# A fourth weight tile at the start, attention values made feature-major, and reordered queues in a two-layer float32 block

## The chip, the cores and the metric

The kernel runs on 1 core of one Trainium2 chip. The time is device microseconds of one launch. The kernel before takes 1545.37 us, the median of 3 runs (1543.23 to 1545.9).

## The reference

Two layers over 256 rows (T) of 1024 float32 features (D). Each layer: an RMS norm, one wide projection of the row, three mixers (MoBA attention, gated linear attention "GLA", mLSTM), each lifted by an up projection and gated, summed, projected by `w_o` and added to the row. Then a second norm and a feed-forward block: dense SwiGLU in layer 0, and in layer 1 a mixture of 8 experts, two per row, by a router.

```python
for l in range(DEPTH):
    h = rmsnorm(x, attn_norm_g[l])
    x = x + hybrid_mixer(h, w_in[l], b_in[l], ...)     # softmax attention | GLA | mLSTM, gates, w_o
    h = rmsnorm(x, ffn_norm_g[l])
    x = x + (swiglu(h, ...) if l % 2 == 0 else moe_swiglu(h, router_w[0], ...))
return rmsnorm(x, final_norm_g)
```

With 256 rows MoBA is plain causal softmax attention: 8 heads of 64.

## The kernel before, in words

**Numbers.** A weight is split in two float32r parts, high (a cast) and low (weight minus high); so is the activation. A product is three matmuls: high by high, high by low, low by high. All weights come as *chunks* of 128 x 2048 float32 (1 MB), in the order of use. A chunk is loaded by two transfers of 512 KB on the sync queue (`load`, `moe_loads`), cast on the scalar engine (ACT) into `w_hi` (`split_to` L1179, in the experts `split_moe` L1241), subtracted on the vector engine (DVE) into `w_lo` (L1521, in the experts L1665), and used by TensorE (PE): 24 matmuls of 512 columns in the dense part (`chunk`, L655 and L665; L644 is its form with 256 columns), 12 per chunk in the experts (L1100, L1111). `w_hi` and `w_lo` have 3 slots each (RS), the raw weights 3 slots in the dense part (RM, `raw_m`) and 11 in the experts (RE, `raw_m` and `late`). In the dense part the sync queue may load chunk g only when chunk g-3 has been split (`sp.wait_ge(lo_ready, g - RM + 1)`).

**Order.** Each engine has its own program, written out by hand, and runs it in order; a wait blocks all that stands behind it on that engine. `ahead(l, name, c)` on ACT and DVE means: split weights up to two chunks beyond chunk c of that unit. Engines wait on semaphores: `lo_ready` counts low parts, `full[b]` and `drained[b]` count the fills and the readings of PSUM bank b. The table `FILL`, made by `fills`, fixes which bank each result takes; PE's `claim` waits until the bank's last content is drained.

**Start.** The first two chunks (0 and 1, unit `mq`) come in five pieces (`PIECES`), each piece of x transposed (`front`, L439) followed by its weight piece (L441), all on the sync queue. Then chunk 2, `cols`, x by rows (`load_x`) and, after a wait for the first low part, chunk 3 into slot 0. The GpSimd (POOL) program waits for the last piece and then asks for biases, small weights and rope tables.

**A mixer layer.** PE runs units mq, mk, mv, gqk, gv, gr, lq, lk, lv, lo, g0 and so on, with small attention steps between them. MoBA: scores (L701), softmax without division, `prob_transposes` (L709), `prob_values` (L719, L725: rows of queries out, 64 columns per head), division by the row sums on DVE (`moba_rows`, L1630), and later `y_transposes(l, 0)` (L690), whose result is split into `yT_hi`/`yT_lo`. The mLSTM convolution (`conv_taps`, L1648) is 12 DVE operations for each of two halves, followed by a Silu on ACT.

**Router and experts.** Between the last `wo'` chunk and the first expert stand the logits (L1000, L1002), `lgT`, the ranks (L1035) and fillers (`keep_warm`, L1008, PSUM bank 3). DVE computes the picks, writes the selection matrix (`select`, L2013), the low rows (`rows_lo`, L1992), then `count_picks` (L1980 to L1984), which reads the `rank` bank for the last time at L1982. PE's `gather` (L1054) then writes 8 banks (`GBANKS`, the first is bank 0). The expert loop goes over `MS`: gate/up chunks ("gu", i, 0 and 1) and down chunks ("dn", i). After "gu" i is full, ACT writes the Silu (L1455), DVE `hid` (L2072), PE transposes it (L1078), ACT and DVE split it (L1460, L2083). `late_split` puts the split of chunk m+2 on DVE behind `hid` at "gu" i < 2. `gates_of_picks` (L1999 to L2007) stands at the first expert's third down chunk.

Of the kernel before, what the change touches and what calls it, by code (L numbers as in the profile page):

```python
# [12 lines left out]
def program(nc, x, front_d, b_in, cols_d, w_small_d, gate_w, dense_d, experts_d,  # L13
# [10 lines left out]
    P = 128  # L24
# [74 lines left out]
    for l in range(L):  # L99
        if l:  # L100
            fills(l, "norm", A4)
        for tag, banks in (
                ("mq", (0, 1)), ("rb", (5,)), ("mk", (2, 3)), ("small", (4,)), ("mv", (0, 1)),
                ("qkT", A4), ("gqk", (2, 3)), ("gv", (0, 1)), ("s0", A4), ("gr", (2, 3)), ("s1", A4),
                ("lq", (0, 1)), ("ga", (7,)), ("lk", (2, 3)), ("pT0", A4), ("lv", (0, 1)), ("pv0", (4, 5)),
# [12 lines left out]
    fills(1, "logits", (0,))  # L118
    fills(1, "lgT", (1,))
    fills(1, "rank", (0,))  # L120
# [68 lines left out]
    with ctx:  # L189
# [189 lines left out]
        p_ready = sem("probs_ready")  # L379
        y_ready = sem("y_gla_mlstm_ready")  # L380
# [44 lines left out]
        def _(sp):  # L425
# [11 lines left out]
            for i, (k0, k1) in enumerate(PIECES):  # L437
                c = slice(KT + k0 * T if k0 else 0, KT + k1 * T)
# [48 lines left out]
        def _(pool):  # L487
# [29 lines left out]
            pool.wait_ge(piece_in[-1], 16)  # L517
# [79 lines left out]
        def _(pe):  # L597
# [81 lines left out]
            def y_transposes(l, br):  # L679

                if br:
                    pe.wait_ge(y_ready, (2 * l + br) * NT)
                else:
                    await_drained(l, "pv1", 0)
                    await_drained(l, "pv1", 1)
# [18 lines left out]
            def prob_transposes(l, g):  # L704
                pe.wait_ge(p_ready, 2 * l + g + 1)
                for hh in range(4):
                    b = claim(l, f"pT{g}", hh)
                    for j in range(3):
                        ins = nc.tensor.transpose(ps[:, b, j * P:(j + 1) * P], sc[:, g, hh, j * P:(j + 1) * P],  # L709
                                                  ident[:, :])  # L710
                    done(ins, l, f"pT{g}", hh)

            def prob_values(l, g):
                for hh in range(4):
                    await_drained(l, f"pT{g}", hh)
                b0, b1 = claim(l, f"pv{g}", 0), claim(l, f"pv{g}", 1)
                for hh in range(4):
                    h = 4 * g + hh
                    ins = mm(ps[:, b0, hh * HD:(hh + 1) * HD], pT[:, hh, 2 * P:3 * P], vm[:, 0, h * HD:(h + 1) * HD],  # L719
                             start=True, stop=True)  # L720
                done(ins, l, f"pv{g}", 0)
                for hh in range(4):
                    h = 4 * g + hh
                    for j in range(2):
                        ins = mm(ps[:, b1, hh * HD:(hh + 1) * HD], pT[:, hh, j * P:(j + 1) * P],  # L725
                                 vm[:, j, h * HD:(h + 1) * HD], start=(j == 0), stop=(j == 1))
                done(ins, l, f"pv{g}", 1)
# [78 lines left out]
            for l in range(L):  # L806
# [41 lines left out]
                prob_transposes(l, 0)  # L848
# [17 lines left out]
                y_transposes(l, 0)  # L866
# [13 lines left out]
                for i in range(2):  # L880
                    await_drained(l, "yT0", i)
# [130 lines left out]
            pe.wait_ge(pair_ready, 1)  # L1012
            lg_bank = claim(1, "logits")
            keep_warm(5)
# [138 lines left out]
        def _(act):  # L1153
# [82 lines left out]

            def split_moe(pas, m):
# [6 lines left out]
            A(y0, ident[:, 0:2], ACT.Copy)  # L1244
            for k in range(KT):
# [7 lines left out]
            for l in range(L):  # L1253
# [33 lines left out]
                ahead(l, "gr")  # L1287
# [33 lines left out]
                ahead(l, "lo")  # L1321
# [3 lines left out]
                for u in range(2):  # L1325
                    act.wait_ge(conv3, 2 * l + u + 1)
                    A(mqk[:, 4 * u:4 * u + 4, :], mqk[:, 4 * u:4 * u + 4, :], ACT.Silu).then_inc(mqk_ready, 1)
# [6 lines left out]
                for i in range(2):  # L1334
                    hi_of(l, "yT0", i, yT_hi)
# [11 lines left out]
                ahead(l, "up0")  # L1347
                await_drained(l, "mb", 1)
# [141 lines left out]
        def _(dve):  # L1490
# [124 lines left out]
            def row_sums(l, g):  # L1615
# [3 lines left out]
                note(V.reciprocal(sums[:, g, :, :], sums[:, g, :, :]))  # L1619
# [5 lines left out]

            def moba_rows(l, g):
                settle()
                for t in range(NT):
                    b = await_full(l, f"pv{g}", t)
                    tt(ytok[:, t, g * T:(g + 1) * T].rearrange("p (h n) -> p h n", h=4),  # L1630
                       ps[:, b, 0:T].rearrange("p (h n) -> p h n", h=4),
                       sums[:, g, t, :].unsqueeze(2).to_broadcast([P, 4, HD]), ALU.mult).then_inc(drained[b], 1)
# [46 lines left out]
            for l in range(L):  # L1679
# [73 lines left out]
                soft_scores(l, 1)  # L1753
                row_sums(l, 0)
# [33 lines left out]
                conv_taps(l, 1)  # L1788
# [429 lines left out]
```

## Time and profile before

| | |
|---|---|
| median of 3 runs | 1545.37 us |
| the profiled execution | 1545.86 us |
| its span, first to last instruction | 1544.1 us (1.8 us lie around it) |
| PE busy, share of the span | 1516.3 us, 98% |
| PE weight loads | 1267.2 us, 82% |
| DVE busy | 1231.9 us, 80% |
| ACT busy | 946.0 us, 61% |
| POOL busy | 37.9 us, 2% |
| DMA | 412.71 MB, mean 267 GB/s |

Matmuls are pipelined: one of 512 columns is shown with 390 ns, but the starts of two in a row lie 0.23 us apart. So PE's busy share hides small stalls, and they are read from the starts: a start later than the cadence of its row group is a stall. Times in the views are us from the start of the span; in a timeline row the first number is the start, the second the time covered, and the bracket gives the idle time ahead of it with what ended it.

### The profile page before, as it was taken

Reading aid. Unit: us, or ns where it says so; the run is one execution under the profiler, and the core shown is the slowest. Engines: PE = TensorE matmul, PEld = TensorE weight load, DVE = VectorE, ACT = ScalarE, POOL = GpSimd, SP = SyncE. Lnnn points to the kernel's source line nnn. Section 1 sums busy time; section 2 is a strip of 40 time slices with the busy share of each in tenths; the row PEclk is TensorE's granted clock in tenths of the full one; section 3 lists DMA queues with packets and bytes.
Section 4 is the critical chain, followed back from the end, with each engine's and each line's share of the span. In section 5 each row is a group of like instructions: output and inputs, shape, how many; then the busy total and the mean of one; then the engine's idle time right before and its main releaser. Section 6 shows DMA issues by size and latency. Waiting matters only on the chain.

```text
span 1544.1 us, 19326 instructions
## 1 busy us (share of the span) xinstructions
PE 1516.3 (98%) x7534; PEld 1267.2 (82%) x7534; DVE 1231.9 (80%) x1218; ACT 946.0 (61%) x881; POOL 37.9 (2%) x69
## 2 busy tenths in 40 slices
PE   8999999999999999999899999999999999999996
PEld 6898888888888898888678888888888888888885
DVE  5778876655547688866699998989989999899996
ACT  6347534544435356534677777777777777777775
POOL 2000000000000000001000000000000000000000
PEclk9999999999999999999999999999999999999998
DMA  8544545455554455546799998999989999999980
GB/s 297 212 166 141 191 175 191 174 189 191 191 191 166 177 184 183 180 164 242 308 367 377 348 372 327 360 376 347 372 321 372 370 353 355 341 363 370 351 305 29
DMA packets 114802, 412.71 MB, mean 267 GB/s; under 512 B 13264, under 2 KB 13568, under 8 KB 114704
## 3 DMA queue, kind: packets, MB, share of 16 engines
q1 hardware_dynamic: 111872, 402.52, 69.7%
q0 software_dynamic: 2688, 8.61, 1.7%
q8 instruction: 63, 1.03, 0.3%
q14 instruction: 35, 0.29, 0.1%
q10 hardware_dynamic: 144, 0.26, 0.0%
HBM read 410.29 MB, written 1.05 MB: 266 GB/s over the span
## 4 chain that ended last, share of the span: by engine, by line
PE 91%; DVE 5%; ACT 2%; issue 1%; DMA 1%; SPq 0%; DVEq 0%; ACTq 0%
PE ps L1100 31%; PE ps L665 19%; PE ps L1111 14%; PE ps L966 8%; PE ps L655 4%; PE ps L943 4%; PE ps L644 3%; DVE w_lo L1665 2%; PE ps L1054 1%; DMA raw_m<-dense_dram 1%; PE ps L1078 1%; DVE w_lo L1521 1%; PE ps L1063 1%; ACT w_hi L1179 1%; PE ps L623 0%
## 5 line engine op out<-in xcount | busy, mean ns | idle before, releaser
L1665 DVE TENSOR_TENSOR w_lo<-late,w_hi 128x2048 fp32r<-128x2048 f32 x192 | 438.1, 2290 | 38.7 <-ACT w_hi L1241 38.6
L1241 ACT CAST w_hi<-late 128x2048 fp32r<-128x2048 f32 x192 | 367.3, 1913 | 44.3 <-PE ps L1100 44.3
L1521 DVE TENSOR_TENSOR w_lo<-raw_m,w_hi 128x2048 fp32r<-128x2048 f32 x115 | 262.6, 2290 | 130.7 <-ACT w_hi L1179 130.4
L1179 ACT CAST w_hi<-raw_m 128x2048 fp32r<-128x2048 f32 x115 | 218.2, 1906 | 132.7 <-PE ps L665 54.7
L1100 PE MATMUL ps<-w_hi,hT_hi 128*128 128x512 f32 x704 | 281.9, 400 | 2.3 <-DVE w_lo L1665 2.3
L1100 PE MATMUL ps<-w_hi,hT_lo 128*128 128x512 f32 x704 | 274.9, 390 | 0.0
L1100 PE MATMUL ps<-w_lo,hT_hi 128*128 128x512 f32 x704 | 274.6, 390 | 0.0
L665 PE MATMUL ps<-w_hi,hT_hi 128*128 128x512 f32 x464 | 183.6, 396 | 3.5 <-DVE w_lo L1521 3.5
L1665 DVE TENSOR_TENSOR w_lo<-raw_m,w_hi 128x2048 fp32r<-128x2048 f32 x72 | 165.4, 2298 | 24.2 <-ACT w_hi L1241 24.2
L665 PE MATMUL ps<-w_hi,hT_lo 128*128 128x512 f32 x464 | 181.0, 390 | 0.0
L665 PE MATMUL ps<-w_lo,hT_hi 128*128 128x512 f32 x464 | 180.7, 389 | 0.0
L1100 PEld LDWEIGHTS ps<-w_hi,hT_hi 128*128 128x128 f32 x704 | 132.2, 188 | 29.4 <-DVE w_lo L1665 4.5
L1100 PEld LDWEIGHTS ps<-w_hi,hT_lo 128*128 128x128 f32 x704 | 132.1, 188 | 28.2
L1100 PEld LDWEIGHTS ps<-w_lo,hT_hi 128*128 128x128 f32 x704 | 132.5, 188 | 25.1
L1241 ACT CAST w_hi<-raw_m 128x2048 fp32r<-128x2048 f32 x72 | 137.8, 1914 | 21.3 <-PE ps L1100 14.4
L1111 PE MATMUL ps<-w_hi,yT_hi 128*128 128x512 f32 x352 | 137.4, 390 | 0.9 <-DVE w_lo L1665 0.9
L1111 PE MATMUL ps<-w_hi,yT_lo 128*128 128x512 f32 x352 | 137.3, 390 | 0.0
L1111 PE MATMUL ps<-w_lo,yT_hi 128*128 128x512 f32 x352 | 137.0, 389 | 0.0
L665 PEld LDWEIGHTS ps<-w_hi,hT_hi 128*128 128x128 f32 x464 | 87.1, 188 | 22.4 <-DVE w_lo L1521 5.0
L665 PEld LDWEIGHTS ps<-w_hi,hT_lo 128*128 128x128 f32 x464 | 87.1, 188 | 18.6
L665 PEld LDWEIGHTS ps<-w_lo,hT_hi 128*128 128x128 f32 x464 | 87.2, 188 | 17.2
L1460 ACT CAST yT_hi<-ps 128x256 fp32r<-128x256 f32 x88 | 32.8, 373 | 80.5 <-PE ps L1078 80.5
(343 smaller groups left out, 2158.2 us busy)
## 6 DMA issues: line engine op xcount, KB each, us to landing
late<-experts_dram SPq DMA_DIRECT2D x384, 512.0 KB, 4.7
raw_m<-dense_dram SPq DMA_DIRECT2D x233, 512.0 KB, 4.0
raw_m<-experts_dram SPq DMA_DIRECT2D x144, 512.0 KB, 4.4
bias<-b_in_dram POOLq DMA_DIRECT2D x26, 256.0 KB, 4.8
xt<-x_dram SPq DMA_DIRECT2D x4, 256.0 KB, 8.2
tmp<-front_dram SPq DMA_DIRECT2D x3, 256.0 KB, 6.3
out_dram<-xn SPq DMA_DIRECT2D x3, 256.0 KB, 4.2
tmp<-w_small_dram POOLq DMA_DIRECT2D x2, 320.0 KB, 5.1
```

The lines of the kernel that those rows point to most:

```text
L644: ins = mm(ps[:, b, (m % 2) * T:(m % 2 + 1) * T], wsp[a][:, s, kk * W + m * P:kk * W + (m + 1) * P], hT[r][:, k, :], start=(k == 0 and m % ...
L655: ins = mm(ps[:, b, :], yT[a][:, k, t * P:(t + 1) * P], wsp[r][:, s, k * W:(k + 1) * W], start=(k == 0 and pa == 0), stop=(k == 3 and pa = ...
L665: ins = mm(ps[:, b, :], hT[a][:, k, t * P:(t + 1) * P], wsp[r][:, s, kk * W:(kk + 1) * W], start=(k == 0 and pa == 0), stop=(k == KT - 1 a ...
L943: ins = mm(ps[:, b, :], yT[a][:, 2 * (i % 2) + kk, t * P:(t + 1) * P], wsp[r][:, s, kk * D + h * W:kk * D + (h + 1) * W], start=(i == 0 an ...
L966: ins = mm(ps[:, b, :], hT[a][:, k, t * P:(t + 1) * P], wsp[r][:, s, kk * W:(kk + 1) * W], start=(k == 0 and pa == 0), stop=(k == KT - 1 a ...
L1100: ins = mm(ps[:, b, :], hT[a][:, k, x * P:(x + 1) * P], wsp[r][:, s, kk * W:(kk + 1) * W], start=(k == 0 and pa == 0), stop=(k == KT - 1 a ...
L1111: ins = mm(ps[:, b, :], yT[a][:, y + kk, 0:P], wsp[r][:, s, kk * D + h * W:kk * D + (h + 1) * W], start=(i == 0 and kk == 0 and pa == 0), ...
L1179: copy(w_hi[:, g % RS, :], slot_raw(g, False)).then_inc(hi_ready, 1)
L1241: copy(w_hi[:, m % RS, :], slot_raw(m, True)).then_inc(hi_ready, 1)
L1460: copy(yT_hi[:, r:r + 2, 0:P], ps[:, b, 0:2 * P].rearrange("p (m n) -> p m n", m=2))\
L1521: tt(w_lo[:, g % RS, :], slot_raw(g, False), w_hi[:, g % RS, :], ALU.subtract)\
L1665: tt(w_lo[:, m % RS, :], slot_raw(m, True), w_hi[:, m % RS, :], ALU.subtract).then_inc(lo_ready, 1)
```

## The change

On the sync queue, chunk 3 gets a place of its own (`mqk_flat`, a part of `late` that is unused then), and is asked for right behind chunk 2, ahead of `cols` and x by rows. The x columns of pieces 2 to 4 are issued from ACT's queue. POOL waits for chunk 3 instead of the last piece. In the mixers, DVE divides the probabilities before they are transposed, PE computes the values feature-major in one bank per half, and the transposes of y and the DVE rows after them go; some splits, `conv_taps(1)` and the Silu after it change their place. At the end of layer 0's feed-forward block one split on DVE moves behind the last `yT_lo`. Around the router, `logits` and `rank` take other banks and `keep_warm` comes ahead of the claim. In the experts `late_split` is narrowed, and `gates_of_picks` and half of `add_rows` move.

```diff
@@ fills
-  ("lq", (0, 1)), ("ga", (7,)), ("lk", (2, 3)), ("pT0", A4), ("lv", (0, 1)), ("pv0", (4, 5)),
-  ("pT1", (6, 7, 4, 5)), ("lo", (2, 3)), ("pv1", (4, 5)), ("g0", (0, 1)), ("lc", (6,)),
-  ("gs", (4, 5, 7, 6)), ("yT0", (4, 5)), ("g0'", (2, 3)), ("go", (4, 5)), ("mb", (6, 7)),
+  ("lq", (0, 1)), ("ga", (7,)), ("lk", (2, 3)), ("pT0", A4), ("lv", (0, 1)), ("pv0", (4,)),
+  ("pT1", (6, 7, 5, 4)), ("lo", (2, 3)), ("pv1", (5,)), ("g0", (0, 1)), ("lc", (6,)),
+  ("gs", (4, 5, 7, 6)), ("g0'", (2, 3)), ("go", (4, 5)), ("mb", (6, 7)),
-    fills(1, "logits", (0,))
+    fills(1, "logits", (2,))
     fills(1, "lgT", (1,))
-    fills(1, "rank", (0,))
+    fills(1, "rank", (4,))
@@ slot_raw
+            if n == RM and not moe:
+                return mqk_flat
@@ block.sync
             for i, (k0, k1) in enumerate(PIECES):
-                sp.dma_start(front[:, c], front_d[:, c]).then_inc(xT_in[i], 16)
+                if i < 2:
+                    sp.dma_start(front[:, c], front_d[:, c]).then_inc(xT_in[i], 16)
...
-                    if g >= RM:
+                    if g > RM:
                         sp.wait_ge(lo_ready, g - RM + 1)
                     load(g)
-                    if g == 2:
+                    if g == RM:
                         sp.dma_start(cols[:, :, :], ...)
                         load_x(0)
                         load_x(1)
@@ block.gpsimd
-            pool.wait_ge(piece_in[-1], 16)
+            pool.wait_ge(raw_in[0], 32)
@@ block.tensor
-                pe.wait_ge(p_ready, 2 * l + g + 1)
-                for hh in range(4):
+                pe.wait_ge(p_scaled, 2 * l + g + 1)
+                for hh in heads:
...
-                    ins = mm(ps[:, b0, hh * HD:(hh + 1) * HD], pT[:, hh, 2 * P:3 * P], vm[:, 0, ...])
-                for hh in range(4):
-                    for j in range(2):
-                        ins = mm(ps[:, b1, hh * HD:(hh + 1) * HD], pT[:, hh, j * P:(j + 1) * P], vm[:, j, ...])
+                    mm(ps[p0:p0 + HD, b, c0:c0 + T], vm[:, 0, v], pT[:, hh, 0:T], start=True, stop=False)
+                    ins = mm(ps[p0:p0 + HD, b, c0 + P:c0 + T], vm[:, 1, v], pT[:, hh, T:T + P], ...)
...
                 prob_values(l, 0)
-                prob_transposes(l, 1)
-                unit(l, "lo")
+                prob_transposes(l, 1, range(3))
+                chunk(l, "lo", 0)
+                prob_transposes(l, 1, (3,))
+                chunk(l, "lo", 1)
                 prob_values(l, 1)
...
                 chunk(l, "g0'", 0)
-                y_transposes(l, 0)
                 chunk(l, "g0'", 1)
...
+            keep_warm(10)
             lg_bank = claim(1, "logits")
-            keep_warm(5)
@@ block.scalar
+            for i in range(2, len(PIECES)):
+                act.dma_start(front[:, c], front_d[:, c]).then_inc(xT_in[i], 16)
...
-                ahead(l, "gr")
+                ahead(l, "lq", 0)
...
+                hi_of(l, "pv0", 0, yT_hi[:, 0:2, :])
                 ahead(l, "lv")
                 probs_out(1)
-                ahead(l, "lo", 0)
+                ahead(l, "lo")
                 act.wait_ge(gla_cum, l + 1)
...
-                ahead(l, "lo")
+                hi_of(l, "pv1", 0, yT_hi[:, 2:4, :])
...
-                for u in range(2):
-                    act.wait_ge(conv3, ...)   # and the Silu
+                conv_silu(l, 0)
...
                 ahead(l, "up0")
+                conv_silu(l, 1)
@@ block.vector
-                note(V.reciprocal(sums[:, g, :, :], sums[:, g, :, :]))
+                link(V.reciprocal(sums[:, g, :, :], sums[:, g, :, :]))
+                tt(sc[:, g, :, 0:T], sc[:, g, :, 0:T], ..., ALU.mult)
+                tt(sc[:, g, :, T:T + P], sc[:, g, :, T:T + P], ..., ALU.mult).then_inc(p_scaled, 1)
-            def moba_rows(l, g): ...
...
                 soft_scores(l, 1)
+                ahead(l, "lq", 0)
                 row_sums(l, 0)
...
-                moba_rows(l, 0)
+                lo_of(l, "pv0", 0, yT_hi[:, 0:2, :], yT_lo[:, 0:2, :])
                 ahead(l, "lv")
-                probs_out(l, 1)
                 biased(l, "lv", ...)
                 ahead(l, "lo", 0)
+                probs_out(l, 1)
+                ahead(l, "lo")
...
-                conv_taps(l, 1)
-                ahead(l, "lo")
                 biased(l, "lo", lambda t: lo[:, t, :])
-                moba_rows(l, 1)
+                lo_of(l, "pv1", 0, yT_hi[:, 2:4, :], yT_lo[:, 2:4, :])
...
-                for i in range(2):
-                    lo_of(l, "yT0", i, yT_hi, yT_lo)
                 ahead(l, "g0'")
                 biased(l, "g0'", lambda t: gates[:, 1, t, :])
+                conv_taps(l, 1)
...
-                            split_to(min(2 * NU + n + 2, LAYER_BASE[1]))
+                            split_to(min(2 * NU + n + 2, LAYER_BASE[1] - 1))
...
+                    split_to(LAYER_BASE[1])
...
-                    late_split = kind == "gu" and c == 1 and i < 2
+                    late_split = e > 0 and (kind, i, c) == ("gu", 0, 1)
...
+                    if pas == 0 and m == 1:
+                        gates_of_picks()
                     if kind == "gu" and c == 1:
...
+                        if e and i == 1:
+                            add_rows(pas, e - 1, 0)
...
-                    if e and (kind, i, c) == ("gu", 1, 0):
-                        add_rows(pas, e - 1, 0)
                     if (e, kind, i) == (0, "dn", 2):
                         if pas == 0:
-                            gates_of_picks()
```

## Rows read from the trace of the kernel before

**Rows 1.** The waits of PE, by line: total us, times, longest.
```profile
PE ps L665 <- DVE w_lo L1521: 3.5, 2, 2.4
PE ps L1100 <- DVE w_lo L1665: 2.3, 9, 0.3
```

**Rows 2.** Timeline of ACT over the first 30 us.
```profile
9.12 0.62 ACT L1251 CAST w_hi<-raw_m 128x512 fp32r<-128x512 f32 x1 [0.73 <-DMA raw_m<-dense_dram]
...
15.79 1.91 ACT L1179 CAST w_hi<-raw_m 128x2048 fp32r<-128x2048 f32 x1 [1.10 <-DMA raw_m<-dense_dram]
...
24.03 1.91 ACT L1179 CAST w_hi<-raw_m 128x2048 fp32r<-128x2048 f32 x1 [6.34 <-DMA raw_m<-dense_dram]
```

**Rows 3.** Timeline of the sync queue at the start.
```profile
11.49 27.29 SPq L435 DMA_DIRECT2D raw_m<-dense_dram  x12
```

**Rows 4.** DMA queues from 18 to 24 us: packets, MB, share of 16 engines.
```profile
q1 hardware_dynamic: 355, 1.28, 55.4%
q0 software_dynamic: 354, 1.09, 47.9%
```

**Rows 5.** Timeline of PE in layer 0's mixers: small steps between units.
```profile
138.29 1.00 PE L719 MATMUL ps<-late 128*128 128x64 f32 x8
139.13 1.95 PE L725 MATMUL ps<-late 128*128 128x64 f32 x16
...
161.20 1.03 PE L690 MATMUL ps<-ident,ytok 128*128 128x128 f32 x8
161.99 0.48 PE L665 MATMUL ps<-w_hi,hT_hi 128*128 128x512 f32 x1
...
194.28 0.59 PE L889 MATMUL ps<-late 128*128 128x256 f32 x2
...
196.81 0.48 PE L665 MATMUL ps<-w_hi,hT_hi 128*128 128x512 f32 x1
```

**Rows 6.** Timelines of DVE and PE in the same layer.
```profile
139.18 5.07 DVE L1648 SCALAR_TENSOR_TENSOR late<-late,cols 128x256 f32<-128x256 f32 x12
...
171.04 1.22 DVE L1825 TENSOR_REDUCE st<-tmp 128x8 f32<-128x1024 f32 x1 [2.56 <-ACT tmp L1341]
...
184.03 1.29 DVE L1849 TENSOR_TENSOR ytok<-ytok,late 128x512 f32<-128x512 f32 x2
...
187.91 1.04 PE L690 MATMUL ps<-ident,ytok 128*128 128x128 f32 x8
```

**Rows 7.** Timeline of DVE and PE at the end of layer 0's feed-forward block.
```profile
456.35 2.29 DVE L1521 TENSOR_TENSOR w_lo<-raw_m,w_hi 128x2048 fp32r<-128x2048 f32 x1 [1.24 <-ACT w_hi L1179]
...
459.30 0.50 PE L943 MATMUL ps<-w_hi,yT_hi 128*128 128x512 f32 x1 [0.70 <-DVE yT_lo L1950]
```

**Rows 8.** Timeline of PE and DVE from the router to the first expert.
```profile
744.79 0.92 PE L1008 MATMUL ps<-chunk_start 128*128 128x256 bf16 x7
745.18 0.69 DVE L2013 TENSOR_TENSOR yT_lo<-bias 128x512 fp32r<-128x512 f32 x1
...
748.51 0.16 DVE L1982 TENSOR_REDUCE bias<-ps 128x1 f32<-128x8 f32 x1
...
748.77 3.75 PE L1054 MATMUL ps<-yT_lo,xn_hi 128*128 128x256 f32 x16 [3.06 <-issue]
...
755.32 0.47 PE L1100 MATMUL ps<-w_hi,hT_hi 128*128 128x512 f32 x1
```

**Rows 9.** Windows: stretch, length, busy of PE, PEld, DVE, ACT, POOL, then PEclk.
```profile
749.00:755.00 6.00, 6.00 (x31) 6.00 (x32) 1.42 (x3) 4.15 (x5) 0.00 (x0) 0.54 0.89 352
```

**Rows 10.** Timeline of PE: the gather ahead of the third expert.
```profile
940.03 2.08 PE L1054 MATMUL ps<-yT_lo,xn_hi 128*128 128x256 f32 x16
```

**Rows 11.** Timeline of DVE and PE in the experts.
```profile
793.92 0.47 PE L1111 MATMUL ps<-w_hi,yT_hi 128*128 128x512 f32 x1 [0.87 <-DVE w_lo L1665]
...
863.48 4.49 DVE L1665 TENSOR_TENSOR w_lo<-late,w_hi 128x2048 fp32r<-128x2048 f32 x2
...
865.82 0.50 PE L1100 MATMUL ps<-w_hi,hT_hi 128*128 128x512 f32 x1 [0.26 <-DVE w_lo L1665]
```

More of the change, by code:

```diff
@@ L379, in program @@
         p_ready = sem("probs_ready")
+        p_scaled = sem("probs_scaled")
         y_ready = sem("y_gla_mlstm_ready")
@@ L437, in _ @@
             for i, (k0, k1) in enumerate(PIECES):
-                c = slice(KT + k0 * T if k0 else 0, KT + k1 * T)
-                sp.dma_start(front[:, c], front_d[:, c]).then_inc(xT_in[i], 16)
+                if i < 2:
+                    c = slice(KT + k0 * T if k0 else 0, KT + k1 * T)
+                    sp.dma_start(front[:, c], front_d[:, c]).then_inc(xT_in[i], 16)
                 c, d = slice(k0 % 4 * W, ((k1 - 1) % 4 + 1) * W), slice(k0 % 2 * W, ((k1 - 1) % 2 + 1) * W)
@@ L679, in y_transposes @@
             def y_transposes(l, br):
[L681 to L685, printed above, removed]
+                pe.wait_ge(y_ready, (2 * l + br) * NT)
                 for i in range(2):
@@ L715, in prob_values @@
                     await_drained(l, f"pT{g}", hh)
-                b0, b1 = claim(l, f"pv{g}", 0), claim(l, f"pv{g}", 1)
+                b = claim(l, f"pv{g}")
                 for hh in range(4):
[L718 to L721, printed above, removed]
-                for hh in range(4):
-                    h = 4 * g + hh
-                    for j in range(2):
-                        ins = mm(ps[:, b1, hh * HD:(hh + 1) * HD], pT[:, hh, j * P:(j + 1) * P],
-                                 vm[:, j, h * HD:(h + 1) * HD], start=(j == 0), stop=(j == 1))
-                done(ins, l, f"pv{g}", 1)
+                    p0, c0, v = HD * (hh % 2), hh // 2 * T, slice((4 * g + hh) * HD, (4 * g + hh + 1) * HD)
+                    mm(ps[p0:p0 + HD, b, c0:c0 + T], vm[:, 0, v], pT[:, hh, 0:T], start=True, stop=False,
+                       skip_group_check=True)
+                    ins = mm(ps[p0:p0 + HD, b, c0 + P:c0 + T], vm[:, 1, v], pT[:, hh, T:T + P], start=False, stop=True,
+                             skip_group_check=True)
+                done(ins, l, f"pv{g}")
             def gla_scores(l):
@@ L847, in _ @@
                 unit(l, "lk")
-                prob_transposes(l, 0)
+                prob_transposes(l, 0, range(4))
                 unit(l, "lv")
                 prob_values(l, 0)
-                prob_transposes(l, 1)
-                unit(l, "lo")
+                prob_transposes(l, 1, range(3))
+                chunk(l, "lo", 0)
+                prob_transposes(l, 1, (3,))
+                chunk(l, "lo", 1)
                 prob_values(l, 1)
@@ L879, in _ @@
                     done(ins, l, "mb", i)
-                for i in range(2):
-                    await_drained(l, "yT0", i)
+                for g in range(2):
+                    await_drained(l, f"pv{g}")
                 unit(l, "up0")
@@ L1235, in conv_head, with conv_silu @@
                 ins.then_inc(conv0, 1)
+            def conv_silu(l, u):
+                act.wait_ge(conv3, 2 * l + u + 1)
+                A(mqk[:, 4 * u:4 * u + 4, :], mqk[:, 4 * u:4 * u + 4, :], ACT.Silu).then_inc(mqk_ready, 1)
             def split_moe(pas, m):
@@ L1333, in _ @@
                 ahead(l, "g0'", 0)
-                for i in range(2):
-                    hi_of(l, "yT0", i, yT_hi)
                 ahead(l, "g0'", 1)
@@ L1618, in row_sums @@
                 link(V.reduce_sum(sums[:, g, 0, :], sc[:, g, :, T:T + P], AX))
-                note(V.reciprocal(sums[:, g, :, :], sums[:, g, :, :]))
+                link(V.reciprocal(sums[:, g, :, :], sums[:, g, :, :]))
+                tt(sc[:, g, :, 0:T], sc[:, g, :, 0:T], sums[:, g, 1, :].unsqueeze(2).to_broadcast([P, 4, T]), ALU.mult)
+                tt(sc[:, g, :, T:T + P], sc[:, g, :, T:T + P], sums[:, g, 0, :].unsqueeze(2).to_broadcast([P, 4, P]),
+                   ALU.mult).then_inc(p_scaled, 1)
             def probs_out(l, g):
@@ L1624, in probs_out @@
                     V.tensor_copy(pT[:, hh, :], ps[:, b, 0:384]).then_inc(drained[b], 1)
[L1626 to L1632, printed above, removed]
             def conv_rows(l, name):
```

10 lines of the change are left out of this document (4 added, 6 removed).

## Prediction

> **What bounds the kernel now.** I read the page first. PE is busy 98% of the span, DVE 80%, ACT 61%, the chain that ended last is 91% PE. So the time is PE's own work plus the holes in it, and the work of DVE, ACT and the queues costs nothing until PE waits. The list of PE's waits comes second, to find the holes [rows 1]; the timelines around each hole third. In them the idle time of a bracket begins at the modelled end of a matmul (0.39 us after its start), while the next could start after 0.23 us. So a hole costs its shown idle plus 0.16 us: 2.4 is a stall of 2.57, 0.26 one of 0.42. Measured so, all holes of the span sum to some 20 us: about 5.6 in the first 30 us, 0.9 at the end of layer 0, 6 around the router, 4.8 in the experts, the rest crumbs and the tail. The edits touch these four places, and the PE work of the mixers.
>
> **Start.** Chunk 3 is asked for at 11.49, after the first low part, and behind x by rows [rows 3]. It lands at 24.0, ACT casts it at 24.03 and PE stands 2.57 [rows 1, 2]. From 18 to 24 us it shared the DMA engines with POOL's transfers, 1.28 MB to 1.09 [rows 4]. After the change chunk 3 follows chunk 2 directly. Chunk 2 landed at 15.8 [rows 2]; 1 MB at the 0.4 MB/us of that stretch [rows 4] is 2.6 us, so it lands near 18.4, is cast by 20.3 and subtracted by 22.6. PE wants it at 25.7. This stall goes whole: -2.57. Next late is chunk 4, which now stands behind x: it lands by 24 to 26; PE wants it only at 34.6, and ACT and DVE (which still have the norm, and the small weights, now landing some 5 us later, near 27) hand it over at about 32. Cover 2.6 us. Biases are later by as much, also inside that cover.
>
> The x columns from two queues I cost separately. The weights of k = 2 and 3 now have up to 0.5 MB more x ahead of or beside them: at equal shares, as in [rows 4], between 0 and +1.9 us, and I take +1 (larger packets of the weights, less x left). The next hole opens further but ACT then takes 1 us for each k and idled 1.1 us before chunk 2 [rows 2], so +1 is absorbed there: 0. Three issues in front of ACT's first cast (0.4 us each on the sync queue) fall into its wait for x and weights: 0. If the queues together are faster, up to 1.5 more is gained. Start: -2.6, bounds -4.1 and -0.5. A page speaks against this part: the Trainium skill, "DMA: Bandwidth & Descriptors", section "Issuing engines are not separate DMA queues", says that issuing from several engines saves only the issuing time, since all run on the same 16 DMA engines. The shares in [rows 4] agree. By that rule the second queue alone gives nothing and rival (c) loses its first half.
>
> **Mixers, per layer.** Removed: 8 transposes of y, 161.20 to 161.99, 0.79 [rows 5], and about 0.1 for PE's restart after them. The values were 24 records from 138.29 to about 140.9, 2.62 (12 float32 matmuls, two records each); they become 8 matmuls, four of 256 and four of 128 columns. The mLSTM scores are that very mixture: 194.28 to 196.81, 2.53 [rows 5]. So -0.09 twice. One transpose set is split off behind a chunk: +0.1. The split of the lk chunk comes before the row sums and loses a stall of 0.15. Sum -1.1, for two layers -2.2.
>
> New waits: PE waits for scaled probabilities, behind which all its program stands. DVE adds 1.8 us per half (as the subtraction of the same shapes, 1.2 and 0.7) and delivers some 11 us ahead of need. The tight place is later: `conv_taps(1)`, 5.1 us [rows 6], now stands between the g0' biases and the GLA norm. DVE idled 2.56 us there [rows 6], so the chain behind it moves by 2.1 to 2.5. Its end, the gated GLA rows, was done at 185.3 and PE asked at 187.91 [rows 6]: cover 2.6, but PE now comes 1.3 earlier, and DVE's biases with it. I get 0.3 to 0.5 us to spare; if not, up to 1 us per layer is lost. Range 0 to -2.6.
>
> **End of layer 0.** DVE did a split of 2.29 for layer 1 at 456.35, ahead of the low part that PE then waited for, 0.70 idle [rows 7]. Moved behind: -0.86. The moved split is ready near 459.7, PE wants it after 466.
>
> **Router.** PE stops at 745.5 and gathers at 748.77 [rows 8]. The selection is ready at 745.87, the high rows at 744.6. The view says "issue", so no engine is named; but the gather's first bank is 0, where `rank` lay, and its last reader L1982 ends at 748.67, 0.1 before PE starts. I take this bank as the cause. With `rank` in bank 4 the gather can follow the selection: 3.0 us earlier, counting 0.25 for logits that no longer wait for the wo' rows (the ten fillers end at 736.5 instead of logits at 736.74). Second, the granted clock is 0.54 of full in this stretch [rows 9], that is 1.2 GHz instead of 2.4, after PE had idled from 745.5. The 16 matmuls take 3.56 at that clock, the same 16 take 1.91 at the third expert's gather [rows 8, 10]. Without the hole the clock should stay up. Then something else is late: DVE writes low rows and counts until 748.65 and needs 1.3 for the two copies that the first chunk awaits. So the first expert starts at 750.0 instead of 755.32 [rows 8]: -5.3. If the clock falls all the same: -3.1. On that the Trainium skill, "TensorE: Matmul & The Clock Gate", section "HAM oscillation", has the rule that waits of PE re-throttle it; what it would give in each case is the two numbers before.
>
> **Experts.** The stall of 0.42 stands nine times [rows 1]. In experts 1 to 7 it is the same place: DVE does `hid`, then two splits of 4.49 in one [rows 11], and PE waits for the first of them at 865.82. With the narrower `late_split` DVE takes the split when ACT's cast ends (862.1), ends it at 864.3, then `hid` by 864.7 and the added rows (1.2). PE wants `hid` at 865.18, the split right after. No stall, -0.42 seven times: -2.9. The backlog reaches `hid` of i = 2 with 0.25 to spare. In expert 0 two such stalls go, but `gates_of_picks`, 1.55 us, now stands ahead of `hid` 0: PE waits about 1 us for it; net -0.15. Where it stood it made the stall of 0.87 shown, 1.03 [rows 11]: that goes. Experts: -4.1.
>
> **Sum.** -2.6 -2.2 -0.9 -5.3 -4.1 = -15.1. The profiled execution takes 1545.86, so 1530.8; the median of before lies 0.5 lower, so 1530.3.
>
> **Rivals.** (a) The gather is freed but the clock falls again, or PE's "issue" had another cause for part of it. For it: the clock can fall in the thin stretch before, where the logits and ranks have gaps of 0.3 to 1 us. Against it: it held through them before. Costs 2.2 to 5: 1533.
>
> (b) The mixers or the start give nothing: GLA rows come too late in each layer (+1 each), or the delayed pieces of the start push chunk 2 beyond its cover. Against it: the covers above. 1530.3 + 2 to 4: 1533.5.
>
> (c) Faster still: the two queues use DMA time that one left idle at the start (the engines are 80 to 90% busy there), and DVE's order gives more in the experts: 1527.5.
>
> (d) Slower than before: DVE becomes the bound of the experts. It is busy 87 us of an expert's 95. In the new order `hid` 1 stands behind a split; if ACT's cast comes more than 0.5 us later than 862.1, PE waits at the transposes for a split, 2.29, and the added rows push the next split by 1.2 more, 3.5 a time. Seven experts make 24 in place of -2.9. That is 1530.3 + 27.4 = 1557.7. Against it: the order at i of 2 and more is already this one and shows no stall.
>
> (e) The change doesn't do what it says: PE reads none of it because its stalls move on to the next late thing everywhere (DVE's copies, the table loads of ACT): within 0.2%, 1544.
>
> **How the numbers follow.** Forecast 0.58, (a) 0.15, (b) 0.13, (c) 0.08, (d) 0.03, (e) 0.03. The predicted time is the forecast's, 1530.3. The range holds forecast, (a), (b), most of (c): 1526.5 to 1536. Faster by over 0.2% (3.1 us, about what a measurement of this kernel can tell from no change): forecast and (a) to (c), 0.94. Within 0.2%: (e), 0.03. Slower: (d), 0.03.
>
> **What would show it.** Start: ACT's cast of chunk 3 near 18.5 with PE's third unit 2.6 earlier; the cast for k = 2 at 9.1 to 11. Mixers: no L690 in front of the second half of g0', 2.5 us for the values, no PE wait at the GLA transposes. Router: gather at 745.7, 16 matmuls in 1.9, granted clock 1.00. Experts: no wait at the chunk after the second transposes of experts 1 to 7. What would make it wrong: a gather that still starts at 748, a wait on `hid`, or a wait of PE at the GLA transposes in both layers.

## The result, and the profile after

| | before | after |
|---|---|---|
| median | 1545.05 us (1543.23 to 1545.9, 4 runs) | 1528.38 us (1528.12 to 1528.75, 4 runs) |
| ratio | | 0.9894, 95% interval 0.9877 to 0.9911 |
| profiled execution | 1545.86 us, span 1544.1 | 1528.12 us, span 1526.3 |
| PE busy | 1516.3 us, 98% | 1507.4 us, 99% |

16.7 us faster by the medians, 17.8 by the two spans, where I had forecast 15.1. The list of PE's waits of the changed kernel (total us, times, longest), to be read against [rows 1]:

```profile
PE ps L785 <- DVE w_lo L1674: 2.3, 1, 2.3
PE ps L800 <- POOL ident L501: 1.6, 1, 1.6
PE ps L1075 <- DVE ytok L2072: 1.5, 2, 0.8
PE ps L737 <- DVE st L1810: 1.0, 2, 0.5
```

Both waits of [rows 1] are gone: for the low part of a dense chunk (3.5 us) and, nine times, of an expert chunk (2.3). Three others are new or longer: in the first unit (L785), in the first expert (L1075) and at the GLA scores (L737). The next table compares the start of one and the same matmul in both traces. A minus is a gain, and the line numbers are those of the changed kernel:

| stretch, ending at | before | after | gain so far | in the stretch | forecast |
|---|---|---|---|---|---|
| start, first matmul of mv | 37.15 | 35.88 | -1.27 | -1.3 | -2.6 |
| mixers of layer 0, up0 | 171.43 | 167.89 | -3.54 | -2.3 | -1.1 |
| end of layer 0's block | 463.06 | 458.87 | -4.19 | -0.6 | -0.9 |
| mixers of layer 1, up0 | 627.36 | 620.84 | -6.52 | -2.3 | -1.1 |
| router, first expert chunk | 755.32 | 743.56 | -11.76 | -5.2 | -5.3 |
| experts, near PE's end | 1531.40 | 1514.98 | -16.42 | -4.7 | -4.1 |
| PE's end to the span's end | | | -17.8 | -1.4 | 0 |

**Start.** Timeline of ACT, then of DVE, after:

```profile
7.69 0.51 ACT L1253 ACTIVATE hT_hi<-tmp 128x256 fp32r<-128x256 f32 x1 [2.60 <-DMA tmp<-front_dram]
9.04 0.62 ACT L1256 CAST w_hi<-raw_m 128x512 fp32r<-128x512 f32 x1 [0.84 <-DMA raw_m<-dense_dram]
...
16.13 1.91 ACT L1176 CAST w_hi<-raw_m 128x2048 fp32r<-128x2048 f32 x1
18.56 1.91 ACT L1176 CAST w_hi<-late 128x2048 fp32r<-128x2048 f32 x1 [0.53 <-DMA late<-dense_dram]
```

```profile
18.84 2.29 DVE L1524 TENSOR_TENSOR w_lo<-raw_m,w_hi 128x2048 fp32r<-128x2048 f32 x1 [1.51 <-DMA cols<-cols_dram]
```

Chunk 3 is cast at 18.56 instead of 24.03 [rows 2], as forecast (18.5), and PE no longer waits for it. But the second queue has its price ahead of that: the weights of k = 1 are cast at 9.04, and PE stands before the second k. The windows (length, busy of PE, PEld, DVE, ACT, POOL, then PEclk) show what follows:

```profile
5.00:8.00 3.00, 3.00 (x12) 2.26 (x10) 0.69 (x1) 0.40 (x2) 1.55 (x3) 1.00 0.95 325
8.00:11.00 3.00, 0.70 (x4) 0.42 (x3) 1.57 (x3) 1.23 (x4) 0.00 (x0) 0.96 1.03 420
11.00:14.00 3.00, 3.00 (x9) 2.32 (x8) 2.36 (x5) 3.00 (x7) 0.00 (x0) 0.50 1.03 418
```

After 2.3 us of idle time the granted clock is at half, 1.2 GHz, from 11 to 14 us. In the kernel before it was 1.00 in these stretches. DVE, too, idles for a new reason: 1.51 us until `cols` has landed, behind chunk 3 now.

**Mixers.** Timeline of PE, after: the values of the second half and the first matmul of g0, to be read against 138.29 to 140.9 in [rows 5]:

```profile
136.01 0.66 PE L719 MATMUL ps<-late 128*64 128x256 f32 x4
136.50 0.40 PE L721 MATMUL ps<-late 128*64 128x128 f32 x4
136.72 0.65 PE L719 MATMUL ps<-late 128*64 128x256 f32 x4
137.15 0.44 PE L721 MATMUL ps<-late 128*64 128x128 f32 x4
137.52 0.50 PE L669 MATMUL ps<-w_hi,hT_hi 128*128 128x512 f32 x1
```

1.51 us instead of 2.6, where I had put 2.53. It happens four times. And the new wait among the GLA scores, the same in layer 1:

```profile
151.93 0.50 PE L737 MATMUL ps<-late,tmp 64*64 64x64 f32 x6 [0.50 <-DVE st L1810]
```

**Router.** Timeline of PE, after, for [rows 8]:

```profile
739.06 2.17 PE L1051 MATMUL ps<-yT_lo,xn_hi 128*128 128x256 f32 x16 [0.21 <-DVE yT_lo L2011]
741.07 2.17 PE L1051 MATMUL ps<-yT_lo,xn_lo 128*128 128x256 f32 x16
743.56 0.47 PE L1097 MATMUL ps<-w_hi,hT_hi 128*128 128x512 f32 x1 [0.32 <-DVE hT_lo L2025]
```

The gather follows the selection, its first 16 matmuls take 2.01 (start to start) instead of 3.56, and the releaser of the first expert is the copy that I had named. The window of the gather has the clock at 1.00, against 0.54 in [rows 9]:

```profile
738.00:743.00 5.00, 4.79 (x42) 4.43 (x39) 4.82 (x11) 4.93 (x10) 0.00 (x0) 1.00 1.02 406
```

**Experts.** In expert 1 the chunk follows the second transposes with no wait, and PE's waits have none left at L1097 for a low part:

```profile
852.25 0.38 PE L1075 MATMUL ps<-ident,ytok 128*128 128x128 f32 x2
852.39 0.47 PE L1097 MATMUL ps<-w_hi,hT_hi 128*128 128x512 f32 x1
```

In the first expert PE waits 0.84 us for `hid` at 752.81.

### The profile page after: what moved, and what is told of

It is laid out like the page before. It is cut to its first block, busy times and chain, and to the rows that moved or that the text cites. A ratio compares the mean times of both kernels' runs of the same rounds, so it can differ in the third digit from the quotient of the medians.

```text
span 1526.3 us, 19236 instructions
## 1 busy us (share of the span) xinstructions
PE 1507.4 (99%) x7491; PEld 1258.7 (82%) x7491; DVE 1234.3 (81%) x1218; ACT 951.2 (62%) x885; POOL 37.7 (2%) x69
## 4 chain that ended last, share of the span: by engine, by line
PE 91%; DVE 3%; ACT 3%; issue 1%; DMA 0%; SPq 0%; ACTq 0%; DVEq 0%
PE ps L1097 31%; PE ps L669 17%; PE ps L1108 16%; PE ps L963 8%; PE ps L659 4%; PE ps L940 4%; PE ps L648 4%; DVE w_lo L1524 1%; PE ps L1075 1%; PE ps L1051 1%; ACT w_hi L1176 1%; PE ps L1060 1%; PE ps L785 1%; PE ps L627 1%; DMA raw_m<-dense_dram 0%
## 5 line engine op out<-in xcount | busy, mean ns | idle before, releaser
L1097 PE MATMUL ps<-w_hi,hT_hi 128*128 128x512 f32 x704 | 281.9, 400 | 0.3 <-DVE hT_lo L2025 0.3
L1097 PE MATMUL ps<-w_hi,hT_lo 128*128 128x512 f32 x704 | 274.9, 391 | 0.0
L1097 PE MATMUL ps<-w_lo,hT_hi 128*128 128x512 f32 x704 | 274.5, 390 | 0.0
L1097 PEld LDWEIGHTS ps<-w_hi,hT_lo 128*128 128x128 f32 x704 | 132.1, 188 | 28.3
L1097 PEld LDWEIGHTS ps<-w_lo,hT_hi 128*128 128x128 f32 x704 | 132.6, 188 | 25.2
L1097 PEld LDWEIGHTS ps<-w_hi,hT_hi 128*128 128x128 f32 x704 | 132.2, 188 | 25.4 <-issue 0.5
```

Of the source, the lines that this page charges most:

```text
L1097: ins = mm(ps[:, b, :], hT[a][:, k, x * P:(x + 1) * P], wsp[r][:, s, kk * W:(kk + 1) * W], start=(k == 0 and pa == 0), stop=(k == KT - 1 a ...
```

## The experiments

The medians of the variants stand beside 1528.38. That value is from other runs than theirs, and the kernel before had medians of 1545.05, 1544.80, 1544.69 and 1544.13 in the four groups of runs; so what is smaller than 1 us is read from the traces, matmul against matmul, with the start (it varies) taken off. A trace is one execution. The runs take back parts of the change or mend them; none takes back alone chunk 3's own tile, the dropped transposes of y or the moved split at the end of layer 0. What those three gave is read from the pair of traces only.

### All columns of x on one queue

```diff
-                if i < 2:
-                    sp.dma_start(front[:, c], front_d[:, c]).then_inc(xT_in[i], 16)
+                sp.dma_start(front[:, c], front_d[:, c]).then_inc(xT_in[i], 16)
...
-            for i in range(2, len(PIECES)):
-                act.dma_start(front[:, c], front_d[:, c]).then_inc(xT_in[i], 16)
```

> The changed kernel with all columns of x back on the sync queue, each piece ahead of its weights; chunk 3 keeps its own tile. Theory S (the second queue delays the weights of k = 1 from 6.41 to 9.02 us, PE idles until 10.53, and the granted clock then stands at half for 3.41 us): the piece lands near 6.4 again, PE starts k = 1 near 7.9, no record at half clock, mk begins near 20.4 instead of 21.75, time 1.3 us below the changed kernel (about 1527.1). Rival Q (the second queue saves DMA time, and the missing 1.3 us of the start has another cause, such as chunk 3 or the wait for cols): the pieces of k = 4 to 7 land later, chunk 3 too, and the time is equal or 0.5 to 1.5 us above 1528.4.

Measured: 1528.48 (1527.21 to 1529.74). By the time alone theory S falls. The trace, which is of the slowest of the four executions (1529.74), shows that the first half of its mechanism holds (k = 1 is earlier and PE's first hole smaller) and that something else eats the gain. PE (first fence) began the last matmul of the first unit at 19.15, over two us earlier than with two queues (21.52), but then waited 1.82 us for the low part of chunk 2, for which DVE (second) had waited 3 us behind `cols`:

```profile
21.36 0.50 PE L668 MATMUL ps<-w_hi,hT_hi 128*128 128x512 f32 x1 [1.82 <-DVE w_lo L1520]
```

```profile
19.01 2.29 DVE L1520 TENSOR_TENSOR w_lo<-raw_m,w_hi 128x2048 fp32r<-128x2048 f32 x1 [3.01 <-DMA cols<-cols_dram]
```

and the clock fell after this hole in turn (window of the same trace):

```profile
23.00:25.00 2.00, 2.00 (x6) 1.56 (x5) 0.75 (x3) 1.98 (x7) 0.00 (x0) 0.50 0.93 360
```

So mv starts at 37.23 here, later than the changed kernel's 35.88.

### Chunks 2 and 3 subtracted before the wait for cols, one queue

```diff
 (all of the edit above, and on DVE)
+                    split_to(3)
                     dve.wait_ge(c_in, 16)
```

> All columns of x on the sync queue, as in the run with one queue, and DVE subtracts chunks 2 and 3 before it waits for cols. In the run with one queue PE ended the first unit 2 us sooner (19.5 instead of 21.5) but then waited until 21.36 for the low part of chunk 2, whose subtraction stood behind the wait for cols (landed 18.99, before the change 16.0), and the clock stood at half from 23 to 26 us. Theory K (cols behind chunk 3 is the new late thing of the start, and hid what one queue gains): mk begins near 20.4, no half clock, the end of mv's wait 1.5 to 2.5 us sooner than in the changed kernel, time 1526.0 to 1527.0. Rival K2 (chunk 2 itself, landed 16.15, bounds it: cast 18.1, low part 20.3; PE then idles 0.9 us all the same and the clock falls again): 1527.5 to 1528.5.

Measured: 1526.97 (1526.77 to 1527.37), theory K's upper end. DVE takes chunk 2 at 17.68, PE begins mk at 20.03 and mv 1.58 us sooner than in the changed kernel (34.30):

```profile
17.68 2.29 DVE L1520 TENSOR_TENSOR w_lo<-raw_m,w_hi 128x2048 fp32r<-128x2048 f32 x1 [2.11 <-ACT w_hi L1175]
```

```profile
20.03 0.50 PE L668 MATMUL ps<-w_hi,hT_hi 128*128 128x512 f32 x1 [1.10 <-DVE w_lo L1520]
```

K2 has this hole of 1.10 on its side (chunk 2's cast bounds it now), but the clock stays at 1.00 after it. Of the changed start, then, chunk 3's own tile is the gain (by the stall of 2.57 that is gone); the second queue and the place of `cols` each took a part of it back.

### Fillers in the gap, two queues

```diff
+                    if k == 0:
+                        for _ in range(16):
+                            nc.tensor.transpose(ps[:, 7, 0:P], ident[:, :], ident[:, :])
```

> The changed kernel with 16 transposes of the identity (about 1.8 us at 0.11 each) between the matmuls of k = 0 and k = 1 of the first unit, into a bank that nobody reads then. The weights of k = 1 are as late as before (9.02). Theory S1 (of the 1.3 us, some 0.7 to 1.3 come from the half clock after the idle time, not from the lateness itself): granted clock stays 1.00 through 10.8 to 14.2, PE's matmuls of k = 1 and 2 start 0.23 apart, mk begins 0.5 to 1.3 us sooner than 21.75, time 1527.1 to 1527.9. Rival S2 (ACT and DVE, not PE, set the pace of k = 2 to 7, so the slow clock is hidden): clock as in S1, but mk begins at 21.7 and the time is 1528.4 within 0.3.

Measured: 1527.35 (1527.09 to 1527.53). S1: the weights of k = 1 are as late as in the changed kernel (landed 8.99), the clock is now at full speed, and the changed kernel's 21.98 is 21.05 here, mv's 35.88 is 34.99: -0.9. The window that stood at 0.50:

```profile
11.00:14.00 3.00, 3.00 (x14) 2.38 (x13) 2.97 (x6) 3.00 (x7) 0.00 (x0) 1.00 1.02 418
```

Not all of this 0.9 is the clock. `cols` landed earlier here too, and DVE took chunk 2 at 18.36 instead of 18.84. With 18.84 and the 2.29 us of that subtraction, the changed kernel could have begun mk near 21.2 and did at 21.75; so by these rows the slow clock alone cost it about 0.6 us (an estimate), while the medians differ by 1.0.

The Trainium skill, "TensorE: Matmul & The Clock Gate", section "HAM oscillation", has the rule that PE's waits re-throttle it. This pair of traces agrees: the slow stretch follows the hole and is absent where the hole is filled; but the page's loop goes slow after every wait, and here not every wait does it. With the same start and no fillers, the run of the next experiment has the longest first-unit hole of all, 3.08 us, and no slow stretch follows (PE, then two windows):

```profile
10.71 0.47 PE L785 MATMUL ps<-w_hi,hT_hi 128*128 128x512 f32 x1 [3.08 <-DVE w_lo L1674]
```

```profile
8.00:11.00 3.00, 0.29 (x1) 0.30 (x2) 1.57 (x3) 1.43 (x3) 0.00 (x0) 1.00 1.03 419
11.00:14.00 3.00, 3.00 (x14) 2.37 (x13) 2.75 (x6) 3.00 (x8) 0.00 (x0) 1.00 1.02 418
```

Of the six profiled executions with the changed start and no fillers five went to half clock after this hole, of the two with fillers none. So the fillers' effect is likely rather than certain by the traces; the medians support it.

### Two heads in a row on the same half

```diff
-                for hh in range(4):
+                for hh in (0, 2, 1, 3):
                     p0, c0, ... = HD * (hh % 2), ...
```

> The changed kernel with the heads of each half of the attention values in the order 0, 2, 1, 3: the same eight matmuls into the same places, but two heads in a row now write the same 64 partitions (columns of the array) instead of alternating. Theory V (the 1.50 us instead of 2.62 come from heads on the two column halves running side by side): the 16 records take 2.2 to 2.6 us, 0.7 to 1.1 more in each of four places, time 3 to 4 us above the changed kernel (1531.4 to 1532.4). Rival W (the gain comes from fewer instructions or from writing 256 columns at a time): the records take 1.5 us as before and the time is 1528.4 within 0.4.

Measured: 1528.52 (1527.74 to 1528.98). Timeline of PE (the eight matmuls stand for 16 records):

```profile
121.42 0.65 PE L719 MATMUL ps<-late 128*64 128x256 f32 x2
121.91 0.38 PE L721 MATMUL ps<-late 128*64 128x128 f32 x2
122.12 0.65 PE L719 MATMUL ps<-late 128*64 128x256 f32 x4
122.56 0.44 PE L721 MATMUL ps<-late 128*64 128x128 f32 x4
122.83 0.59 PE L719 MATMUL ps<-late 128*64 128x256 f32 x2
123.26 0.38 PE L721 MATMUL ps<-late 128*64 128x128 f32 x2
123.58 1.09 PE L710 MATMUL ps<-ident,tmp 128*128 128x128 f32 x8
```

In the changed kernel heads run as two pairs, 0.71 us each (136.01 to 136.72). Here head 0 alone takes 0.70 (121.42 to 122.12), heads 2 and 1, neighbours on different halves, 0.71 together, and head 3 alone 0.75. A pair costs what one head costs: V holds, and 2.16 against 1.51 us is +0.65 for the one pair that is broken up; all four in a row would take 2.8 (an estimate, four times 0.70). The Trainium skill says it in "TensorE: Matmul & The Clock Gate", section "Part 3: Packing small matmuls — row/col tiling": matmuls whose outputs lie in different column groups run at the same time. This trace agrees, with two 64-column halves in float32. The time missed V's 3 to 4 and is rival W's 1528.4; the records above decide against W, and the trace says where the rest went. The start was 0.65 us better in this execution (mv at 35.23, no slow stretch), and of 4 x 0.65 half was hidden, because the wait at L737 (0.7 in each layer) went as PE came later. From mv to the end PE took 1.15 us more than in the changed kernel.

### The copy of lcol first

```diff
-                ahead(l, "g0", 0)
                 b = await_full(l, "lc")
                 V.tensor_copy(lcol, ps[:, b, 0:16]).then_inc(drained[b], 1)
+                ahead(l, "g0", 0)
```

> The changed kernel with the copy of lcol (bank 6) ahead of the split for g0' on DVE. Theory C (PE's new wait of 0.69 us among the GLA scores, once in each layer, is for bank 6, whose copy stands behind that split, which itself waits 3.5 us for ACT): both stalls go, time 1.4 below the changed kernel (1527.0). Rival C2 (the wait only moves: the masks of the scores come behind two splits, and PE waits later at att_values or at the bank of gs 3): 1528.4 within 0.4.

Measured: 1526.05 (1525.85 to 1527.07), below what theory C gave. The wait is gone in both layers, and from before lo to after the scores PE gains 0.9 us a layer, 0.2 more than the stall. Timeline of DVE: the copy runs when PE delivers, in a gap in which it had idled:

```profile
149.50 0.17 DVE L1809 COPY st<-ps 128x16 f32<-128x16 f32 x1 [3.04 <-PE ps L859]
149.95 4.49 DVE L1524 TENSOR_TENSOR w_lo<-raw_m,w_hi 128x2048 fp32r<-128x2048 f32 x2 [0.27 <-ACT w_hi L1176]
```

### rank back in bank 0

```diff
-    fills(1, "rank", (4,))
+    fills(1, "rank", (0,))
```

> The changed kernel with rank back in bank 0, where the first bank of the gather is; logits stays in bank 2 and the fillers ahead of its claim. Theory R (the bank alone held the gather, and the half clock followed from that hole): the gather starts about 0.1 after the last reader of the bank on DVE, near 741.9 instead of 739.06, the granted clock falls to half in the 16 matmuls after it, first expert 748.5 to 749 instead of 743.56, time 5 us above the changed kernel (1533.4). Rival R2 (the bank gives only the hole, the clock stays up because the fillers stand elsewhere): 3 us above (1531.4). Rival R3 (the moved fillers did it, not the bank): within 0.4 of 1528.4.

Measured: 1532.77 (1532.41 to 1534.69), +4.4, by the trace +4.2 at the first expert. Timeline of PE and a window:

```profile
741.74 3.49 PE L1051 MATMUL ps<-yT_lo,xn_hi 128*128 128x256 f32 x16 [3.06 <-issue]
```

```profile
741.00:745.00 4.00, 3.26 (x16) 3.29 (x17) 0.79 (x4) 1.76 (x3) 0.00 (x0) 0.63 1.02 407
```

The nameless "issue" of 3.06 us is back to the digit [rows 8]. DVE's last read of the bank ended at 741.64, PE starts at 741.74, and the 16 matmuls are slow again. One table entry is the hole and the clock (R; its time, 5 more, was 0.6 too high, and R2's 3 too low). The other 1 us of the router's 5.2 is 0.35 in front of the logits and 0.7 by which the slow clock lasts longer in the kernel before: there all 32 matmuls of the gather need 6.55 us, here 5.81.

### The old order of splits in the experts

```diff
-                    late_split = e > 0 and (kind, i, c) == ("gu", 0, 1)
+                    late_split = kind == "gu" and c == 1 and i < 2
...
-                        if e and i == 1:
-                            add_rows(pas, e - 1, 0)
...
+                    if e and (kind, i, c) == ("gu", 1, 0):
+                        add_rows(pas, e - 1, 0)
```

> The changed kernel with late_split and the place of the first half of add_rows as in the kernel before; gates_of_picks stays where the change put it. Theory X (the order of DVE at the first two gate/up pairs is the whole gain of experts 1 to 7, 0.50 us each): the stall of 0.42 stands again at the chunk after the second transposes, the experts cost 3.5 us more, time 1531.9. Rival X2 (part of it comes from elsewhere, such as the raw weights that become free at other times): the stall comes back, but the time rises by only 1 to 2.5.

Measured: 1531.05 (1530.41 to 1531.38), +2.7; by the traces the experts take 1.13 us less than before instead of 4.66, +3.5. The median lies between theory X (3.5) and X2 (1 to 2.5); the trace decides for X. From its list of waits, and the place of one of them:

```profile
PE ps L1097 <- DVE w_lo L1663: 2.3, 9, 0.3
```

```profile
852.06 0.38 PE L1075 MATMUL ps<-ident,ytok 128*128 128x128 f32 x2
852.69 0.50 PE L1097 MATMUL ps<-w_hi,hT_hi 128*128 128x512 f32 x1 [0.26 <-DVE w_lo L1663]
```

All nine are back. What is left, 1.1, is for the greater part the stall of 1.03 that `gates_of_picks` made at its old place [rows 11].

### gates_of_picks in DVE's idle time

```diff
+                    if pas == 0 and m == 1:
+                        gates_of_picks()
                     if m + 2 < NM and not late_split:
                         split_moe(pas, m + 2)
...
-                    if pas == 0 and m == 1:
-                        gates_of_picks()
```

> The changed kernel with gates_of_picks ahead of the split of chunk 3 instead of behind it, where DVE idles 1.50 us for ACT's cast (747.07 to 748.57). Theory G (its 1.55 us ahead of hid 0 are the stall of 1.01 at 751.6 to 752.8): the stall goes, hid 0 starts near 750.8 instead of 752.33, time 1.0 below the changed kernel (1527.4). Rival G2 (hid 0 would then wait for the split of chunk 3 anyway, or the next hid is late instead): the stall moves on and the time is 1528.4 within 0.3.

Measured: 1527.05 (1526.32 to 1527.94); by the trace -1.0 in the first expert (and 0.4 by a luckier start). Theory G, here DVE's timeline:

```profile
747.86 0.26 DVE L2005 TENSOR_TENSOR bias<-bias 128x16 f32<-128x16 f32 x2
748.27 2.29 DVE L1663 TENSOR_TENSOR w_lo<-late,w_hi 128x2048 fp32r<-128x2048 f32 x1
750.48 0.41 DVE L2072 TENSOR_TENSOR ytok<-ytok,ps 128x256 f32<-128x256 f32 x1
```

### The kernel before, once more

> The kernel before once more, for its profile. The profiled execution of before was a slow one of its own kind (1545.86 of 1542.2 to 1546.1), with 11.5 us between the last matmul and the end where every changed kernel has 10.1 (three output transfers issued over 3.08 us instead of 1.73). If that tail is chance: 10.1 to 10.5 here. If it belongs to the kernel before: 11.5 again. The same for the start: mk begins between 20.0 and 20.7 with chunk 3 cast after 24.0 if the start doesn't vary; else other landing times.

Measured: 1545.74. SP's timeline, first in the profiled execution of before, then here:

```profile
1537.61 3.08 SPq L481 DMA_DIRECT2D out_dram<-xn  x3
```

```profile
1538.85 1.33 SPq L481 DMA_DIRECT2D out_dram<-xn  x3
```

PE ends at 1533.85 and the span at 1544.0: a tail of 10.1, as in every changed kernel. The 11.5 of the first profile was chance, and with it the 1.4 us in the last row of the account. The start varies the other way: the hole in front of chunk 3's low part, 2.59 us here, is followed by a slow stretch (PE, then a window), by none in the first profile, and mv starts at 38.40 instead of 37.15:

```profile
27.94 0.50 PE L665 MATMUL ps<-w_hi,hT_hi 128*128 128x512 f32 x1 [2.59 <-DVE w_lo L1521]
```

```profile
28.00:32.00 4.00, 4.00 (x11) 3.16 (x12) 2.39 (x9) 3.97 (x6) 0.00 (x0) 0.57 0.76 279
```

Against this execution the changed start gains 2.5, against the first one 1.3. The changed start varies too: in the six profiled executions that have it without fillers, mv starts between 35.23 and 36.32.

### All repairs together

Two kernels: fillers, splits before `cols`, lcol's copy and `gates_of_picks` early with two queues; and the same without fillers with one queue.

> The changed kernel (x columns from two queues) with four edits at once: the 16 fillers between k = 0 and k = 1 (measured -1.0), chunks 2 and 3 subtracted before the wait for cols (the stall of 0.55 at the end of the first unit that was left beside the fillers), gates_of_picks ahead of the split of chunk 3 (-1.3), the copy of lcol first (-2.3 by the medians, -1.8 by the traces). If they add up: 1523.6 (1528.4 less 1.0, 0.5, 1.1 and 2.0); mk begins near 20.4, no stall at the GLA scores or in the first expert. If the gains share a cause or a later thing is late in their place: 1525 or more.

Measured: 1523.63 (1523.39 to 1523.8), ratio to before 0.9866 (0.985 to 0.9883).

> As the run with all edits, but with all columns of x on the sync queue and no fillers (its start alone measured 1526.97). Additive: 1526.97 less 1.1 and 2.0, that is 1523.9. Against the run with two queues and fillers this tells whether the second queue is worth anything once the clock is held up: theory S says no (equal within 0.5, or this one faster), rival Q says the two queues win by 0.5 or more.

Measured: 1523.88 (1523.54 to 1524.44), ratio 0.9868 (0.9852 to 0.9884). The gains add up in both, and the times are equal: with the clock held up, the second queue is worth nothing that can be measured. It had the fillers on its side, the single queue needed none (mv starts at 34.22 and 34.49). Both beat the changed kernel by 4.5 us or more. The longest of PE's waits in the first of them; the first two stand in the kernel before as well:

```profile
PE ps L803 <- POOL ident L501: 1.6, 1, 1.6
PE ps L1000 <- DVE hT_lo L1573: 0.8, 1, 0.8
PE ps L1078 <- DVE ytok L2076: 0.6, 1, 0.6
PE ps L785 <- DVE w_lo L1677: 0.6, 1, 0.6
```

## Why the prediction was right, and where it wasn't

**Start, -2.6 forecast, -1.3 found.** The term for chunk 3 was right (cast at 18.56, no stall). The step that failed is "+1 is absorbed there: 0". I had weighed what a late k = 2 and 3 would do, but the piece that was delayed is that of k = 1, with which the x columns of the other queue shared the engines: it landed at 9.02, in the five executions with one queue between 6.2 and 6.9. mk began 1.60 later than before (21.75 against 20.15). The hole was followed by half clock, which I had asked only of the router. The run with fillers started mv 0.9 sooner, the one with one queue and `cols` later 1.6. That chunk 2's low part would stand behind `cols` I had not seen: I listed what the chunk was moved past on the queue, but not that DVE waits for `cols` before it subtracts. The size stays open: against the second execution of the kernel before, whose hole ahead of chunk 3 was followed by half clock, the same start gains 2.5. That comes near the forecast by the clock, which was no part of the sum.

**Mixers, -1.1 forecast, -2.3 each.** The term that was mis-sized is the values: -0.09 a time, taken from the mLSTM scores of the same shapes. Those write all 128 partitions; these write 64 and alternate, and two heads cost one, -1.1 a time. In return "no PE wait" was wrong: the wait at L737, 0.7 a layer (0.9 with what follows it). It was not at the GLA transposes, where I had looked for it, but at `lcol`'s copy: PE reached the scores earlier and DVE's split didn't. The section of the Trainium skill on packing, named above, bears on the first of the two, and the prediction should have weighed it.

**End of layer 0, -0.9 forecast, -0.6.** The wait of [rows 7] went; transposes a little ahead of that place start 0.38 late instead (452.04 in the changed kernel). The view names no releaser for them, so why stays open.

**Router, -5.3 forecast, -5.2.** Right by its steps: the bank behind the nameless wait, the clock, the copies as the next late thing. It is the best tested term, by the run that put the bank back.

**Experts, -4.1 forecast, -4.7.** The order and the place were right, also the 1 us that `gates_of_picks` would cost ahead of `hid` 0. Each of the seven stalls gave 0.50 instead of 0.42: I had counted the gap and not the slower first matmul behind it (0.50 against 0.39 in its record). In expert 0 my "net -0.15" doesn't follow from its own terms, two stalls of 0.42 gone and 1 us come, which make +0.16; with 0.50 for each stall, and the 1.0 that the run with `gates_of_picks` early got back, it was about 0.

**Tail, 0 forecast, -1.4.** Chance, in the profile of before alone. So the kernels' own difference is 16.4 by this pair of traces, near the 16.7 of the medians. Of the rivals (c) was nearest in time, 1527.5, but its first half (two queues use idle DMA time) is refuted; the extra came from the values. That 1528.4 lay within 2 us of 1530.3 is in part luck: a start forecast too good (by 1.3, in this pair) and mixers forecast too poor (by 2.4, both layers) cancelled.

## What to carry to other kernels

When a transfer is moved or given another queue, look at the smallest piece that is due first, and at every engine that waits for what has been pushed behind. A wait named "issue" wants a look at the PSUM bank table: who reads this bank last. And a hole on PE is priced twice, as a hole and as the slow clock that may follow it; fillers save only the second price, here 0.6 to 1.0 us.

## What the runs showed of the hardware

- Float32 matmuls with 64 output partitions each, alternating between partitions 0 to 63 and 64 to 127, run in pairs: 0.71 us for two heads, 0.70 for one.
- The clock after a hole is not decided by its length alone: half speed followed 1.8 us of idle time (one queue), 2.3 (first unit, after) and 2.6 (kernel before, second execution), and did not follow 2.4 (25.9 to 28.3, kernel before, first execution) and 3.1 (heads on the same half). The two executions of the kernel before reach mv 1.25 us apart.
- Two queues at once delay the earlier small transfer: the weights of k = 1 land at 8.8 to 9.7 us in the eight executions with two, at 6.2 to 6.9 in the five with one. The chunk behind the first unit lands no sooner: chunk 2 at about 15.9 with two queues (after), at 15.72 and 16.15 with one.
- Three output transfers of 256 KB took SP between 1.33 and 1.74 us to issue in twelve executions and 3.08 in one, in kernels that don't differ there.
